# Joining the paired fp32 insertions in the mixers: keys, queries and pooling products turned and multiplied two at a time

## The chip, the cores and the metric

The kernel runs on one core of one Trainium2 chip. The metric is the time of the device in microseconds for one execution, as the median of several runs. Everything is float32 at the interface; the large products are made in fp32r from a high and a low part of each operand (x = hi + lo, three products hi·hi, hi·lo, lo·hi), the small ones in plain fp32.

## The reference

A sequence of 256 tokens with 1024 features goes through two layers of one kind and one layer of another. A layer of the first kind is a gated feed-forward block, a mixer, and a second feed-forward block. Cut to what matters here, its mixer is:

```python
z = rms_norm(x, mix_norm) @ w_in
u, q, k, v, gl = split(z)                    # 512, 512, 512, 512, 2048 columns
y_pool = multiscale_pool(u, pool_w, pool_scale)   # per group g of 4: (mean over window - u_g) @ pool_w[g]
q = rope(rms_norm(q)); k = rope(rms_norm(k)) # per head of 64
y_attn = softmax attention of 8 heads(q, k, v)
merged = gates0 * (y_pool @ w_branch_pool) + gates1 * (y_attn @ w_branch_attn)
x = x + merged @ w_out
```

The layer of the second kind has a larger mixer (an mLSTM branch beside a compressed, a selected and a windowed attention) and one feed-forward block with a convolution.

## The kernel before

The program has eight stages in a row: `L0f1 L0 L0f2 L1f1 L1 L1f2 M Mf`. `L0` and `L1` are the mixers of the first kind ("mixers one and two"), `M` is the third mixer, and the others are feed-forward blocks. The weights stream in tiles of 128x1024; ScalarE copies each into its high part (`whi`, L1369), VectorE subtracts it for the low part (`wlo`, L1976), and TensorE multiplies both with the activations `hx`.

Each of the five engines has a program of its own, written out by hand, and they meet in semaphores. Inside a mixer a counter of **beats** sets the order: after every piece of a tile's product each engine's own `tick()` raises its counter and puts in the small work that is listed for that number. The beat only fixes the place in the engine's own instruction stream; it does not make engines meet. In mixers one and two the beats are: 1 to 8 the product for q, 9 to 16 the four blocks for u (two each), 17 to 24 the product for v (four tiles, two token halves each), and 25 onward the gate blocks.

The small work that matters here, in mixers one and two:
- `turn_qk(a, isq)` on TensorE (helper `turn4`, all at L1094): four 128x128 transposes of half a of the rotated keys or queries (`ro`, a part of `gates`) into bank 4+a. It waits until VectorE has added the two parts of the rotation (`rp_add`, L2330). ScalarE moves the result to `kT1` or `qT1` (`turned`, L1700 and L1698).
- `pool_mix(g)` on TensorE (L1137): the pooling product of group g, one fp32 matmul with 256 columns that the chip runs as two matmul instructions, into bank 6 for even g and bank 7 for odd g. It waits until VectorE has the pooled difference (`pl_d`, last written at L2355). ScalarE then writes its high part (L1706, `yphi`), and VectorE its low part (`pool_mix` of VectorE's program, L2359, which raises `yplo`). Since groups 2 and 3 write the banks of groups 0 and 1, TensorE's `pool_mix(g)` for g of 2 or 3 waits for the low part of g - 2:

```python
if g >= 2:
    E.wait_ge("yplo", 4 * l + g - 1)
```

- VectorE's own ticks put the low parts of the pooling at its beats 15, 17, 20 and 23, the additions of the queries at 15 and 16, and the pooled differences at 10, 12, 14 and 16:

```python
if beat in (15, 17, 20, 23):
    pool_mix((15, 17, 20, 23).index(beat))
if beat in (15, 16):
    add(beat - 15, 1)
if beat in (10, 12, 14, 16):
    pool_diff((beat - 10) // 2)
```

- At beat 26 the attention begins on TensorE (`scores`, L1030), which waits for all keys, queries and the last `yplo`.

In the third mixer `turn_q(a)` (beats 24 and 25) does the same for its queries, and `mlstm_turn(a)` (beats 74 and 76) transposes the output of the mLSTM branch into banks 2 and 3; ScalarE and VectorE take it out again at L1842 and L2552, and the first product of the merge waits for both.

Of the kernel before, what the change touches and what calls it, by code (L numbers as in the profile page):

```python
# [228 lines left out]
ML = 46  # L229
# [182 lines left out]
def build_program(nc, x_in, wstream, gains, const_in, par_in, out, cat, pat, plan, addends):  # L412
# [3 lines left out]
    with ExitStack() as ctx:  # L416
# [285 lines left out]
        def pe_program(E):  # L702
# [412 lines left out]
            def mixer1(s, l):  # L1115
                tag = STAGES[s]
                js = jobs1(l)
                beat = 0

                def turn_qk(a, isq):  # L1120
                    if isq:
                        E.wait_ge("rp_add", 4 * l + 2 + a + 1)
                        E.wait_ge("kt_ev", 2 * l + a + 1)
                    else:
                        E.wait_ge("x", 4 * (s - 1) + a + 1)
                        E.wait_ge("rp_add", 4 * l + a + 1)
                        E.wait_ge("ld_c", 16)
                    turn4([ro[:, a * 512 + c * P:a * 512 + c * P + P] for c in range(4)], side[a]).then_inc(sem["qkt_t"], 1)

                def pool_mix(g):  # L1130
                    E.wait_ge("pl_d", PLD(l, g))
                    E.wait_ge("ld_pw", 32 * l + 32)
                    if g >= 2:
                        E.wait_ge("yplo", 4 * l + g - 1)
                    else:
                        E.wait_ge("x", 4 * (s - 1) + 3 + g)
                    e.matmul(side[2 + g % 2][:, 0:S], pw[:, (3 - g) * P:(4 - g) * P], u4[:, 3 - g, 16:16 + S], start=True, stop=True).then_inc(sem["pl_w"], 1)  # L1137

                def before(i):
                    if i < 2:  # L1140
                        E.wait_ge("kt_ev", 2 * l + 2)
                        E.wait_ge("qt_ev", 2 * l + 2)
                        E.wait_ge("yplo", 4 * l + 4)
                    else:
                        E.wait_ge("v_ev", 2 * l + 2)

                def tick():
                    nonlocal beat
                    beat += 1
                    if beat in (10, 12):  # L1150
                        turn_qk((beat - 10) // 2, False)
                    if beat in (22, 24):
                        turn_qk((beat - 22) // 2, True)
                    if beat in (18, 20, 22, 24):
                        pool_mix((beat - 18) // 2)
                    attention(l, beat, 26, js, before)

                first_group(s, f"{tag}k")
                group(f"{tag}q", 512, tick)
                for f in range(4):  # L1160
                    feat_block(T[f"{tag}u{f}"], claim((f"{tag}u", f))[:, 0:S], tick=tick)
                group(f"{tag}v", 512, tick)
                for f in range(KD):
                    for j in range(2):
                        wide_block(T[f"{tag}g{j}{f}"], claim((f"{tag}g", f, j)), tick)
                merge_tail(s, l)

            def mixer2(s):
# [14 lines left out]
                def turn_q(a):  # L1183
                    E.wait_ge("rp_add", 10 + a + 1)
                    E.wait_ge("kc2_ev", 4 * a + 4)
                    turn4([ro[:, a * 512 + c * P:a * 512 + c * P + P] for c in range(4)], side[a]).then_inc(sem["qkt_t"], 1)
# [105 lines left out]
                def tick():  # L1292
                    nonlocal beat
                    beat += 1
                    if 10 <= beat <= 13:
                        turn_k(beat % 2, beat < 12)
                    if beat in (24, 25):
                        turn_q(beat - 24)
                    if beat == 16:
                        gate_rows()  # L1300
                    attention(2, beat, 29, js, before)
                    if beat in (31, 34, 36, 38, 44):
                        compressed((31, 34, 36, 38, 44).index(beat))
                    if beat in range(ML, ML + 24, 6):
                        mlstm_scores((beat - ML) // 6)
                    if beat in MLO:
                        mlstm_out(MLO.index(beat))
                    if beat in (ML + 28, ML + 30):
                        mlstm_turn((beat - ML - 28) // 2)

                def conv_in(f):
                    feat_block(T[f"Mqk{f}"], claim(("Mqk", f))[:, 0:S], tick=tick)
# [32 lines left out]
        def act_program(E):  # L1345
# [329 lines left out]
            def mixer1(s, l):  # L1675
# [32 lines left out]
                def tick():  # L1708
                    nonlocal beat
                    beat += 1  # L1710
                    if beat in (10, 12):
                        turned((beat - 10) // 2, 0)
                    if beat in (22, 24):
                        turned((beat - 22) // 2, 1)
                    if beat in (18, 20, 22, 24):
                        pool_mix((beat - 18) // 2)
                    attention(l, beat, 26, js)

                norm_hi(s, 1)
# [35 lines left out]
            def mixer2(s):  # L1755
# [17 lines left out]
                def turned_q(a):  # L1773
                    E.wait_ge("qkt_t", 8 + a + 1)
                    e.activation(qT2.rearrange("p (k t) -> p k t", t=S)[:, :, a * P:a * P + P], by4(side[a][:, :]), ACT.Copy).then_inc(sem["qt_ev"], 1)
# [68 lines left out]
                def tick():  # L1844
                    nonlocal beat
                    beat += 1
                    if 10 <= beat <= 13:
                        turned_k(beat % 2, beat < 12)
                    if beat == 18:
                        logf()  # L1850
                    if beat in (24, 25):
                        turned_q(beat - 24)
                    if beat == 26:
                        exp_m()
                    if beat in CONV:
                        conv_end(CONV.index(beat))
                    if beat == 28:
                        compressed(0)
                    attention(2, beat, 29, js)
                    if beat in (31, 34):  # L1860
                        compressed((31, 34).index(beat) + 1)
                    if beat == 40:
                        compressed(3)
                    if beat == 44:
                        compressed(4)
                    if beat == ML + 1:
                        mlstm_exp(0)
                    if beat in range(ML + 6, ML + 24, 6):
                        mlstm_exp((beat - ML) // 6)
                    if beat in (ML + 8, ML + 14, ML + 20, ML + 22):  # L1870
                        mlstm_squares((ML + 8, ML + 14, ML + 20, ML + 22).index(beat))
                    if beat in (ML + 28, ML + 30):
                        mlstm_turned((beat - ML - 28) // 2)

                def conv_in(f):
                    tick()
# [90 lines left out]
        def dve_program(E):  # L1967
# [433 lines left out]
            def mixer2(s):  # L2401
# [152 lines left out]
                def tick():  # L2554
# [32 lines left out]
                        mlstm_out(MLO.index(beat))  # L2587
                    if beat == ML + 24:
                        mlstm_gate()
                    if beat in (ML + 28, ML + 30):  # L2590
                        mlstm_lo((beat - ML - 28) // 2)

                def conv_in(f):
                    tick()
# [435 lines left out]
```

## Time and profile before

| | |
|---|---|
| median of 3 runs | 1401.39 us (1401.39 to 1401.51) |
| the profiled execution: its time, its span | 1401.45 us, 1399.7 us |
| TensorE matmul busy | 1394.3 us, 7680 instructions |
| VectorE busy | 1098.7 us (78%) |
| ScalarE busy | 859.1 us (61%) |
| GpSimd busy | 225.9 us (16%) |
| mean granted clock of TensorE | 1.000 |

A matmul's start is recorded and its end is modelled, and the records of neighbours overlap; so the pace of TensorE is read from the distance of starts, not from the durations. Starts are given to 0.01 us. The span is the time between the first and the last instruction, and the execution's own time is 1.75 us more.

### The profile page before, as it was taken

What the parts mean: (1) busy time and instruction counts of PE and PEld (TensorE: products, weight loads), DVE (VectorE), ACT (ScalarE), POOL (GpSimd) and SP (SyncE); (2) the same over time, 40 slices, a digit from 0 to 9 for tenths busy, and PEclk for the clock granted to TensorE, in tenths of its full rate; (3) what the DMA queues carried; (4) which work ended last, traced back from release to release, by engine and by line L of the source; (5) the groups of instructions that cost most, each with busy time, mean ns of one, the idle gap of its engine ahead of it and who ended that gap; (6) DMA issues with size and microseconds to landing.
All of it is one profiled execution on the core that took longest, in us unless ns stands there. A gap on an engine that the chain in (4) does not pass through costs nothing.

```text
span 1399.7 us, 20305 instructions
## 1 busy us (share of the span) xinstructions
PE 1394.3 (100%) x7680; PEld 1195.7 (85%) x7680; DVE 1098.7 (78%) x1665; ACT 859.1 (61%) x1393; POOL 225.9 (16%) x309
## 2 busy tenths in 40 slices
PE   9999999999999999999999999999999999999999
PEld 7888888898888888888888988888888899888887
DVE  7878878776978878788787778788777878688776
ACT  6657655855657656676567646666567765455553
POOL 1112123000111001112050001114149200100000
PEclk9999999999999999999999999999999999999999
DMA  9999755465999859998555557999547336456551
GB/s 369 300 300 281 220 180 183 138 197 185 302 257 289 213 187 299 276 276 226 166 203 181 165 181 270 267 278 260 186 156 256 121 122 225 155 172 220 192 183 59
DMA packets 86329, 304.26 MB, mean 217 GB/s; under 512 B 11724, under 2 KB 11864, under 8 KB 86232
## 3 DMA queue, kind: packets, MB, share of 16 engines
q1 hardware_dynamic: 72120, 251.84, 51.4%
q0 software_dynamic: 13824, 50.34, 18.9%
q8 instruction: 61, 1.00, 0.3%
q10 hardware_dynamic: 288, 0.79, 0.1%
q14 instruction: 36, 0.29, 0.1%
HBM read 301.87 MB, written 1.06 MB: 216 GB/s over the span
## 4 chain that ended last, share of the span: by engine, by line
PE 99%; DMA 0%; DVE 0%; ACT 0%; issue 0%; POOL 0%; ACTq 0%; POOLq 0%
PE bank L752 18%; PE bank L759 9%; PE bank L706 9%; PE bank L707 9%; PE bank L708 9%; PE bank L931 5%; PE bank L930 5%; PE bank L934 5%; PE bank L736 4%; PE bank L743 4%; PE bank L737 4%; PE bank L773 4%; PE bank L778 3%; PE bank L774 3%; PE bank L726 1%; PE bank L1030 1%
## 5 line engine op out<-in xcount | busy, mean ns | idle before, releaser
L1976 DVE TENSOR_TENSOR wlo<-raw,whi 128x1024 fp32r<-128x1024 f32 x409 | 492.5, 1231 | 12.3 <-ACT whi L1369 12.2
L1369 ACT ACTIVATE whi<-raw 128x1024 fp32r<-128x1024 f32 x409 | 417.8, 1049 | 20.3 <-PE bank L708 13.8
L752 PE MATMUL bank<-hx,whi 128*128 128x512 f32 x1088 | 267.2, 392 | 0.0
L752 PEld LDWEIGHTS bank<-hx,whi 128*128 128x128 f32 x1088 | 200.8, 188 | 41.6 <-issue 2.0
L706 PE MATMUL bank<-whi,hid 128*128 128x512 f32 x536 | 211.1, 394 | 0.0
L707 PE MATMUL bank<-wlo,hid 128*128 128x512 f32 x536 | 209.2, 390 | 0.0
L708 PE MATMUL bank<-whi,hid 128*128 128x512 f32 x536 | 208.8, 389 | 0.0
L759 PEld LDWEIGHTS bank<-hx,wlo 128*128 128x128 f32 x1088 | 142.9, 191 | 7.6
L759 PE MATMUL bank<-hx,wlo 128*128 128x256 f32 x1088 | 145.2, 282 | 0.0
L1976 DVE TENSOR_TENSOR wlo<-gates,whi 128x1024 fp32r<-128x1024 f32 x96 | 116.2, 1220 | 7.6 <-ACT whi L1369 7.0
L708 PEld LDWEIGHTS bank<-whi,hid 128*128 128x128 f32 x536 | 100.6, 188 | 21.4
L1369 ACT ACTIVATE whi<-gates 128x1024 fp32r<-128x1024 f32 x96 | 100.5, 1056 | 28.6 <-PE bank L708 13.5
L706 PEld LDWEIGHTS bank<-whi,hid 128*128 128x128 f32 x536 | 100.8, 188 | 18.9
L707 PEld LDWEIGHTS bank<-wlo,hid 128*128 128x128 f32 x536 | 100.9, 188 | 18.4
L1398 ACT ACTIVATE hid<-prod 128x256 fp32r<-128x256 f32 x78 | 32.6, 418 | 121.9 <-DVE prod L2286 58.6
L2710 POOL DMA_DIRECT2D gates<-w_dram x64 | 55.8, 872 | 290.1 <-DVE wlo L1976 290.1
L773 PE MATMUL bank<-whi,hx 128*128 128x512 f32 (+1 forms) x220 | 86.3, 394 | 0.1
L774 PE MATMUL bank<-whi,hx 128*128 128x512 f32 (+1 forms) x220 | 84.0, 383 | 0.0
L2665 POOL TENSOR_SCALAR small<-small 128x1 f32<-128x1 f32 x15 | 10.7, 715 | 403.0 <-ACT arena L1384 403.0
L930 PE MATMUL bank<-whi,yhi 128*128 128x512 f32 x192 | 75.2, 392 | 0.0
L931 PE MATMUL bank<-whi,ylo 128*128 128x512 f32 x192 | 74.9, 390 | 0.0
L778 PE MATMUL bank<-wlo,hx 128*128 128x512 f32 (+1 forms) x220 | 66.2, 383 | 0.0
(297 smaller groups left out, 2413.8 us busy)
## 6 DMA issues: line engine op xcount, KB each, us to landing
raw<-w_dram SPq DMA_DIRECT2D x414, 512.0 KB, 4.6
gates<-w_dram POOLq DMA_DIRECT2D x64, 512.0 KB, 8.1
gates<-w_dram SPq DMA_DIRECT2D x32, 512.0 KB, 5.0
arena<-w_dram POOLq DMA_DIRECT2D x32, 512.0 KB, 8.9
arena<-w_dram SPq DMA_DIRECT2D x16, 512.0 KB, 5.3
gain<-g_dram SPq DMA_DIRECT2D x7, 512.0 KB, 3.4
out_dram<-x SPq DMA_DIRECT2D x4, 256.0 KB, 2.0
par<-p_dram SPq DMA_DIRECT2D x1, 867.0 KB, 10.1
```

The costliest lines, as they stand in the source:

```text
L706: e.matmul(psum, shi, mhi, start=first, stop=False, skip_group_check=True)
L707: e.matmul(psum, shi, mlo, start=False, stop=False, skip_group_check=True)
L708: return e.matmul(psum, slo, mhi, start=False, stop=last, skip_group_check=True)
L752: e.matmul(b[:, :], hi_of(j)[:, k * P:k * P + P], hx[:, k * 2 * S:k * 2 * S + 2 * S], start=k == 0, stop=False, skip_group_check=True)
L759: ins = e.matmul(b[:, 0:S], lo_of(j)[:, k * P:k * P + P], hiT(k), start=False, stop=k == KD - 1, skip_group_check=True)
L773: e.matmul(b[:, 0:n], hiT(k, a * P, a * P + P), w, start=k == 0, stop=False, skip_group_check=True)
L774: e.matmul(b[:, 0:n], loT(k, a * P, a * P + P), w, start=False, stop=False, skip_group_check=True)
L778: ins = e.matmul(b[:, 0:n], hiT(k, a * P, a * P + P), w, start=False, stop=k == KD - 1, skip_group_check=True)
L930: e.matmul(b[:, :], sh(k), half(hi_of(j), k), start=k == 0 and n not in (2, 4), stop=False, skip_group_check=True)
L931: e.matmul(b[:, :], sl(k), half(hi_of(j), k), start=False, stop=False, skip_group_check=True)
L1369: e.activation(hi_of(t), raw_of(t), ACT.Copy).then_inc(sem["w_hi"], 1)
L1976: e.tensor_tensor(lo_of(t), raw_of(t), hi_of(t).bitcast(F32), ALU.subtract).then_inc(sem["w_lo"], 1)
```

## The change

In mixers one and two the two transposes of the keys move from beats 10 and 12 to beat 12, those of the queries from 22 and 24 to 22, and the four pooling products from 18, 20, 22 and 24 to 18 (groups 0 and 1) and 22 (groups 2 and 3). Six insertions of fp32 work into the stream of fp32r products become three. TensorE and ScalarE get the new places; the program of VectorE is as it was, and so is GpSimd's. In the third mixer `turn_q` moves from beats 24 and 25 to 25 on both engines, and `mlstm_turn` from 74 and 76 to 76, here on TensorE, ScalarE and VectorE.

```diff
@@ TensorE, mixers one and two
-                    if beat in (10, 12):
-                        turn_qk((beat - 10) // 2, False)
-                    if beat in (22, 24):
-                        turn_qk((beat - 22) // 2, True)
-                    if beat in (18, 20, 22, 24):
-                        pool_mix((beat - 18) // 2)
+                    if beat in (12, 22):
+                        for a in range(2):
+                            turn_qk(a, beat == 22)
+                    if beat in (18, 22):
+                        for g in range(2):
+                            pool_mix(2 * (beat == 22) + g)
@@ TensorE, mixer three
-                    if beat in (24, 25):
-                        turn_q(beat - 24)
+                    if beat == 25:
+                        for a in range(2):
+                            turn_q(a)
...
-                    if beat in (ML + 28, ML + 30):
-                        mlstm_turn((beat - ML - 28) // 2)
+                    if beat == ML + 30:
+                        for a in range(2):
+                            mlstm_turn(a)
@@ ScalarE, mixers one and two
-                    if beat in (10, 12):
-                        turned((beat - 10) // 2, 0)
-                    if beat in (22, 24):
-                        turned((beat - 22) // 2, 1)
-                    if beat in (18, 20, 22, 24):
-                        pool_mix((beat - 18) // 2)
+                    if beat in (12, 22):
+                        for a in range(2):
+                            turned(a, beat == 22)
+                    if beat in (18, 22):
+                        for g in range(2):
+                            pool_mix(2 * (beat == 22) + g)
@@ ScalarE, mixer three: turned_q at 25 alone, mlstm_turned at ML + 30 alone
@@ VectorE, mixer three: mlstm_lo at ML + 30 alone
```

Since the beats are numbers, the rows show best what moves. TensorE in mixer one, before: the transposes of the queries (L1094, banks 4 and 5) and the pooling products of groups 2 and 3 (L1137, banks 6 and 7) stand on both sides of the last pair of token halves of v (L773, L774, L778).

```order
854 L1094 MATMUL bank4<-cst,gates 128x128 [waits s_kt_ev,s_rp_add]
855 L1094 MATMUL bank4<-cst,gates 128x128 x3
856 L1137 MATMUL bank6<-arena 128x256 [waits s_yplo,s_pl_d]
```

```order
868 L1094 MATMUL bank5<-cst,gates 128x128 [waits s_kt_ev,s_rp_add]
869 L1094 MATMUL bank5<-cst,gates 128x128 x3
870 L1137 MATMUL bank7<-arena 128x256 [waits s_yplo,s_pl_d]
871 L752 MATMUL bank2<-hx,whi 128x512 [waits s_w_hi,s_u_ev]
```

The same place in the changed kernel:

```order
854 L1094 MATMUL bank4<-cst,gates 128x128 [waits s_kt_ev,s_rp_add]
855 L1094 MATMUL bank4<-cst,gates 128x128 x3
856 L1094 MATMUL bank5<-cst,gates 128x128 [waits s_kt_ev,s_rp_add]
857 L1094 MATMUL bank5<-cst,gates 128x128 x3
858 L1137 MATMUL bank6<-arena 128x256 [waits s_yplo,s_pl_d]
859 L1137 MATMUL bank7<-arena 128x256 [waits s_yplo,s_pl_d]
860 L773 MATMUL bank0<-whi,hx 128x512 [waits s_w_hi]
```

The second half of the queries and group 3, with its wait for `yplo`, now stand twelve matmuls of v earlier.

VectorE in mixer one, the same in both kernels (rows of the one before). L2359 with bank 6 or 7 is what raises `yplo`:

```order
665 L2359 SCALAR_TENSOR_TENSOR ylo<-bank6,par,yhi 128x256 [waits s_yphi]
666 L2330 TENSOR_TENSOR gates<-gates 128x512 [waits s_rp_c,s_rp_s] x2
667 L2349 TENSOR_TENSOR arena<-arena 128x271 [waits s_pl_d,s_u_ev]
668 L2353 TENSOR_TENSOR arena<-arena 128x2 [waits s_pl_d]
669 L2355 SCALAR_TENSOR_TENSOR arena<-arena 128x256 [waits s_pl_d]
670 L1976 TENSOR_TENSOR wlo<-raw,whi 128x1024 [waits s_w_hi]
671 L2359 SCALAR_TENSOR_TENSOR ylo<-bank7,par,yhi 128x256 [waits s_yphi]
```

Nothing moved here: the low part of group 1 (bank 7) still comes behind the additions of the queries, the pooled difference of group 3 and one split of a weight tile.

## Rows read from the trace of the kernel before

**Rows 1.** The page: TensorE's busy time, and the chain that ended last, by engine

```profile
PE 1394.3 (100%) x7680; PEld 1195.7 (85%) x7680; DVE 1098.7 (78%) x1665; ACT 859.1 (61%) x1393; POOL 225.9 (16%) x309
...
PE 99%; DMA 0%; DVE 0%; ACT 0%; issue 0%; POOL 0%; ACTq 0%; POOLq 0%
```

**Rows 2.** The waits of TensorE: us in total, times, longest

```profile
PE bank L1333 <- POOL arena L2840: 1.0, 1, 1.0
PE bank L726 <- DVE arena L1994: 0.9, 1, 0.9
```

**Rows 3.** Timeline of TensorE, blocks for u in mixer one: start us, us

```profile
213.45 0.60 PE L1094 MATMUL bank<-cst,gates 128*128 128x128 f32 x4
...
216.76 0.60 PE L1094 MATMUL bank<-cst,gates 128*128 128x128 f32 x4
...
220.07 0.28 PE L736 MATMUL bank<-hx,whi 128*128 128x256 f32 x1
...
222.95 0.40 PE L773 MATMUL bank<-whi,hx 128*128 128x512 f32 x1
```

**Rows 4.** Timeline of TensorE, the product for v in mixer one

```profile
225.70 0.59 PE L1137 MATMUL bank<-arena 128*128 128x256 f32 x2
...
228.90 0.59 PE L1137 MATMUL bank<-arena 128*128 128x256 f32 x2
...
232.10 0.60 PE L1094 MATMUL bank<-cst,gates 128*128 128x128 f32 x4
...
232.54 0.60 PE L1137 MATMUL bank<-arena 128*128 128x256 f32 x2
...
235.71 0.60 PE L1094 MATMUL bank<-cst,gates 128*128 128x128 f32 x4
...
236.14 0.60 PE L1137 MATMUL bank<-arena 128*128 128x256 f32 x2
```

**Rows 5.** Timeline of TensorE, two token halves of q in mixer one

```profile
205.14 0.39 PE L773 MATMUL bank<-whi,hx 128*128 128x512 f32 x1
...
207.86 0.39 PE L773 MATMUL bank<-whi,hx 128*128 128x512 f32 x1
```

**Rows 6.** VectorE in mixer one: three rows of its timeline, one stretch by engines (after span: PE, PEld, DVE, ACT, POOL busy)

```profile
224.58 0.92 DVE L2355 SCALAR_TENSOR_TENSOR arena<-arena 128x256 f32<-128x256 f32 x1
...
230.71 1.28 DVE L2330 TENSOR_TENSOR gates<-gates 128x512 f32<-128x512 f32 x2
...
234.05 0.47 DVE L2359 SCALAR_TENSOR_TENSOR ylo<-bank,par,yhi 128x256 fp32r<-128x256 f32 x1
...
222.00:240.00 18.00, 18.00 (x96) 15.20 (x96) 17.54 (x27) 10.03 (x16) 3.94 (x6) 1.00 0.47 158
```

**Rows 7.** The same place in mixer two: timelines of TensorE and VectorE

```profile
735.82 0.60 PE L1094 MATMUL bank<-cst,gates 128*128 128x128 f32 x4
...
737.75 0.48 DVE L2359 SCALAR_TENSOR_TENSOR ylo<-bank,par,yhi 128x256 fp32r<-128x256 f32 x1
```

**Rows 8.** Start of the program: timelines of TensorE and VectorE

```profile
1.03 3.57 PE L1333 MATMUL bank<-arena 128*128 128x128 f32 x15 [1.03 <-POOL arena L2840]
...
5.75 0.83 PE L1333 MATMUL bank<-arena 128*128 128x128 f32 x6
...
8.89 0.73 PE L794 MATMUL bank<-whi,hx 128*128 128x512 f32 x2 [0.18 <-DVE hx L2640]
...
8.15 0.69 DVE L2640 CAST hx<-bank 128x512 fp32r<-128x512 f32 x1
```

**Rows 9.** Mixer three: ScalarE and TensorE behind the query transposes, VectorE and TensorE behind the mLSTM ones

```profile
1062.05 0.60 ACT L1775 ACTIVATE arena<-bank 128x512 f32<-128x512 f32 x1 [0.32 <-PE bank L1094]
...
1065.01 0.93 PE L1030 MATMUL bank<-arena 64*128 64x128 f32 x8
...
1162.90 0.69 DVE L2552 TENSOR_TENSOR ylo<-bank,yhi 128x512 fp32r<-128x512 f32 x1 [1.63 <-ACT yhi L1842]
...
1167.54 0.64 PE L743 MATMUL bank<-yhi,wlo 128*128 128x256 f32 x4
```

More of the change, by code:

```diff
@@ L1850, in tick @@
                         logf()
-                    if beat in (24, 25):
-                        turned_q(beat - 24)
+                    if beat == 25:
+                        for a in range(2):
+                            turned_q(a)
                     if beat == 26:
@@ L1871, in tick @@
                         mlstm_squares((ML + 8, ML + 14, ML + 20, ML + 22).index(beat))
-                    if beat in (ML + 28, ML + 30):
-                        mlstm_turned((beat - ML - 28) // 2)
+                    if beat == ML + 30:
+                        for a in range(2):
+                            mlstm_turned(a)
                 def conv_in(f):
@@ L2589, in tick @@
                         mlstm_gate()
-                    if beat in (ML + 28, ML + 30):
-                        mlstm_lo((beat - ML - 28) // 2)
+                    if beat == ML + 30:
+                        for a in range(2):
+                            mlstm_lo(a)
                 def conv_in(f):
```

## The prediction

> **What bounds the kernel.** I read the page first, then TensorE's waits, then the timelines of TensorE and VectorE side by side around the moved work. TensorE is busy for the whole span and makes up 99% of the chain that ended last [rows 1]; it waits for another engine only in the first 9 us [rows 2]. So time goes away only if TensorE issues faster, and every wait the change puts on it is added in full: nothing behind it has slack to take it back. Whatever ScalarE and VectorE do sooner or later counts only where TensorE then stands still.
>
> **What an insertion costs now.** The change removes no matmul; it can only save what TensorE loses at the seams between fp32r products and fp32 work. The seams are read from distances of starts.
> - A block for u without an insertion takes 222.95 - 220.07 = 2.88 us; with four transposes it takes 216.76 - 213.45 = 3.31 [rows 3]. The insertion costs 0.43 us, some 0.109 per transpose.
> - Two token halves of q take 207.86 - 205.14 = 2.72 us [rows 5]. For v, with one pooling product in front, they take 228.90 - 225.70 = 3.20 [rows 4], so the product costs 0.48. Behind transposes the same product and pair take 235.71 - 232.54 = 3.17 [rows 4], so 0.44 of it are its own two matmuls.
> - Transposes directly in front of a pooling product take 232.54 - 232.10 = 0.44 us [rows 4], the same as alone, although they have one seam less. The whole insertion of beat 22 costs 235.71 - 232.10 - 2.72 = 0.89, against 0.43 + 0.48 = 0.91 for the two apart. A seam is therefore worth 0.02 us for a transpose group, and at most 0.05 for a pooling product.
>
> **Terms of the sum, gains.** In each of mixers one and two three seams go: one at beat 10 (0 to 0.02), one at beat 20 (0.02 to 0.05), one at beat 24 (0.02 to 0.05). That is about 0.1 us per mixer. What is saved ahead of beat 22 only makes TensorE arrive sooner at the wait below and is lost there. In mixer three two seams go, 0 to 0.1 us together; I take 0.03.
>
> **Terms of the sum, waits.** The new places are checked one by one.
> - Beat 12, keys. Both halves are added before 216.76, since TensorE turned both by then without waiting, so no wait. VectorE's next need of the first half comes behind both.
> - Beat 18, pooling 0 and 1. Group 1 stood 3.2 us later. Its difference is finished at 224.58 + 0.92 = 225.50 [rows 6]; TensorE is ready for it at 225.70 + 0.22 = 225.92 [rows 4]. No wait, with 0.4 us to spare.
> - Beat 22, second half of the queries. The additions are ready at 230.71 + 1.28 = 231.99 [rows 6]; TensorE wants the second at 232.10 + 0.44 = 232.54 [rows 4]. No wait, 0.5 us to spare.
> - **Beat 22, pooling 3.** It writes bank 7 and must wait until VectorE has taken the low part of group 1 out of it. That instruction starts at 234.05 and ends at 234.05 + 0.47 = 234.52 [rows 6]. Before, TensorE came there at 236.14 and found it done. Beat 22 itself begins where it did, since as much work stands in front of it as before. Now pooling 3 comes after eight transposes and pooling 2: 232.10 + 8 x 0.109 + 0.44 = 233.41. Will VectorE be there sooner, since ScalarE can now deliver the high part of group 1 three microseconds earlier? No: VectorE is 17.54 us busy in the 18.00 us around it [rows 6], its order did not move, and what stands ahead of L2359 are query additions, the difference of group 3 and a weight split, none of them released by moved work. It is the length of its own queue that sets 234.52.
>
> The latency from VectorE's end to TensorE's start is 8.89 - (8.15 + 0.69) = 0.05 us [rows 8]. So pooling 3 starts at 234.58 instead of 233.41: a standstill of 1.17 us. The end result, by the next fixed point: behind pooling 3 now come the last two token halves of v, 235.71 - 232.54 = 3.17 us with the product [rows 4], so the gate blocks begin at 237.75; before they began 0.43 behind 236.14, at 236.57. The mixer loses **1.18 us**, the seam of beat 24 already in it. The first weight load behind a standstill cannot be fetched under the previous matmul. That may add 0 to 0.15; I take 0.05.
>
> Mixer two has the same picture: its beat 22 starts at 735.82, its VectorE instruction ends at 737.75 + 0.48 = 738.23 [rows 7]; 738.28 - (735.82 + 0.87 + 0.44) = 1.15 us.
>
> What is behind the waiting matmul: v's last pair, then the gates, all 1.2 us later, and ScalarE, which stands at L1706 for group 3 about 1 us and splits the next weight tile later. That tile is four tiles ahead of TensorE's use, and VectorE comes to its low part only about 4 us later, so TensorE does not see it. Nor does VectorE wait at its remaining two low parts: ScalarE has group 2 by about 234.2 and group 3 by 235.7, VectorE's turns come at about 235.6 and 238.2. The attention's start needs the last low part at 238.7, TensorE comes at about 240.6.
>
> Mixer three. The queries: ScalarE takes the second half out at 1062.05 [rows 9]; with the first half now directly ahead of it that becomes 1062.1, and it is wanted at 1065.01 [rows 9]. The mLSTM turns: VectorE's second low part starts at 1162.90 and ends at 1163.59 [rows 9]; both halves now pass through ScalarE and VectorE one behind the other, which moves this to about 1163.9, and the first merge product, whose low-part matmuls are at 1167.54 [rows 9] and whose high-part ones start about 1 us before, wants it at 1166.6. Some 2.7 us to spare. Both cost nothing; if a cover were gone, it would cost the lateness, at most 0.3.
>
> **Sum**, against the profiled execution's 1401.45 us: +1.18 +1.15 +2 x 0.05 -0.03 = +2.4 us, 1403.85. The median of the runs is 0.06 lower, which gives **1403.8 us**, 0.17% more. A measurement of this kernel tells about 0.2% (2.8 us) from no change, so this is within no change, near its upper edge.
>
> **Rivals.**
> - *Seams only, no standstill* (chance 0.07). If the standstill did not occur, because VectorE's queue ran earlier than I think, the seams would give -0.2 to -0.3 us: 1401.2. Against it: VectorE's busy share and unchanged order. For a gain beyond 0.2% eight seams would each have to be worth 0.35 us; rows 3 and 4 give 0.05.
> - *The standstill is dearer by its restart, or VectorE is later* (0.20). Each 0.2 us per mixer adds 0.4; from 0.2 more per mixer on the result is slower by over 0.2%. With 0.3 more each: +3.0, 1404.4.
> - *The clock falls* (0.05), the mechanism on the other side. Place: beat 22, where TensorE now does 0.87 us of transposes, 0.44 of pooling, then 1.17 of nothing, in one row. At the program's start 128-column matmuls come 3.15 / 14 = 0.22 us apart for the first 15, and (0.83 - 0.27) / 5 = 0.11 apart for the last six [rows 8]: the first ran at the pace of 1.2 GHz, the last at that of 2.4, and the slow pace held for some 4 us. If the clock fell for as long in both mixers, half of it lost each time, 2 x 2 us more: 1407.8. It decides from a single fall on (+4.4). Against it: the granted clock is 1.00 in the stretch around beat 22 [rows 6] with 0.9 us of insertion in it, and TensorE stood still 0.9 us and 0.18 us between 6.6 and 8.9 [rows 2, 8], and the pair of 512-column matmuls behind took 0.73 us, not the 1.2 of the slow pace. On this the Trainium skill speaks against the change: "TensorE: Matmul & The Clock Gate", Part 4, says that transposes do not keep the clock gate open the way matmuls do, and its section on why this matters warns of idle gaps between bursts of matmuls. By that page transposes and standstill together would count as one gap, and the time would be the 1407.8 of this rival; the trace agrees in so far as it can only for the short gap at the start, where there was no fall, and no row here shows transposes and a standstill in one.
>
> **How the numbers follow.** My forecast, the standstill of 1.1 to 1.3 us in each of mixers one and two, has 0.68, and its own range is 1403.4 to 1404.2. The range 1402.4 to 1404.8 adds most of the dearer restart and the case that one mixer's wait is half as long, and leaves out seams alone and the clock. Slower by over 0.2% (above 1404.2): the dearer restart (0.16 of it) and the clock (0.05), with the edge of my own case, 0.24. Faster by over 0.2%: 0.02. Within: 0.74.
>
> **What the profile will show.** Right: in TensorE's waits a new row, L1137 released by VectorE's L2359 (or its new line number), 2 times, 1.1 to 1.3 us each, at about 233.4 and 737.1; the fp32r pace before and behind as now; no wait at beats 12 and 18; mixer three without one. VectorE's two low parts of group 1 at the same times as now within 0.1 us. Wrong: no such wait; a wait of the attention's first scores; an fp32r pace of 0.45 us per 512 columns behind beat 22; or a span that differs from 1399.7 by more than the two waits.

## The result, and the profile after

| | before | after |
|---|---|---|
| median (lowest to highest, runs) | 1401.57 us (1401.39 to 1401.96, 16) | 1404.35 us (1403.87 to 1404.74, 16) |
| the profiled execution: time, span | 1401.45, 1399.7 us | 1404.03, 1402.2 us |
| mean granted clock | 1.000 | 1.000 |

The ratio is 1.0019, with a 95% interval of 1.0013 to 1.0026: 2.78 us more, where the prediction said 1403.8 us and a range of 1402.4 to 1404.8. It is just under the 0.2% that it called no change. It also lies above 1404.2, the top of my own forecast's range: 0.18 us of that is the kernel before, which takes 1401.57 here and 1401.39 in the runs I started from; the rest is looked for below.

The page of the changed kernel, TensorE's busy time and the chain that ended last, answers to [rows 1]. TensorE has no more work than before, but the chain now passes through VectorE. Its 4% are not the cost: from each standstill the chain runs back over a long stretch in front of it, 35 us in mixer one and most of it VectorE's.

```profile
PE 1394.9 (99%) x7680; PEld 1195.8 (85%) x7680; DVE 1097.9 (78%) x1665; ACT 859.5 (61%) x1393; POOL 226.0 (16%) x309
...
PE 94%; DVE 4%; issue 1%; ACT 1%; DMA 0%; POOL 0%; DVEq 0%; ACTq 0%; POOLq 0%
```

The waits of TensorE in the changed kernel (us in total, times, longest) answer to [rows 2]. One row is new, the foreseen one. Lines below the edit have moved: L2363 is the L2359 of before.

```profile
PE bank L1137 <- DVE ylo L2363: 2.2, 2, 1.1
PE bank L1335 <- POOL arena L2845: 1.0, 1, 1.0
PE bank L726 <- DVE arena L1998: 0.6, 1, 0.6
```

TensorE's timeline in mixer one (start us, us, and in brackets the idle time before) answers to [rows 4]:

```profile
225.48 1.02 PE L1137 MATMUL bank<-arena 128*128 128x256 f32 x4
...
231.84 1.03 PE L1094 MATMUL bank<-cst,gates 128*128 128x128 f32 x8
232.71 0.60 PE L1137 MATMUL bank<-arena 128*128 128x256 f32 x2
234.43 0.67 PE L1137 MATMUL bank<-arena 128*128 128x256 f32 x2 [1.12 <-DVE ylo L2363]
234.75 0.58 PE L773 MATMUL bank<-whi,hx 128*128 128x512 f32 x1
...
237.70 1.07 PE L752 MATMUL bank<-hx,whi 128*128 128x512 f32 x4
```

And VectorE's timeline there answers to [rows 6]:

```profile
230.46 1.28 DVE L2334 TENSOR_TENSOR gates<-gates 128x512 f32<-128x512 f32 x2
231.66 0.43 DVE L2353 TENSOR_TENSOR arena<-arena 128x271 f32<-128x271 f32 x1
...
232.32 0.43 DVE L2359 SCALAR_TENSOR_TENSOR arena<-arena 128x256 f32<-128x256 f32 x1
232.67 1.22 DVE L1980 TENSOR_TENSOR wlo<-raw,whi 128x1024 fp32r<-128x1024 f32 x1
233.80 0.48 DVE L2363 SCALAR_TENSOR_TENSOR ylo<-bank,par,yhi 128x256 fp32r<-128x256 f32 x1
```

VectorE goes through its list as before, 0.25 us earlier, since the whole execution runs 0.22 us ahead after a shorter opening. The low part ends at 233.80 + 0.48 = 234.28. TensorE was ready for pooling 3 at 232.71 + 0.44 = 233.15 and starts it at 234.43: it lost 1.28 us. (The row says 1.12, since the modelled end of the matmul in front lies 0.16 later than the point where the next could have started.) Then 234.75 - 234.43 = 0.32 us pass to the start of the next product. In the kernel before, with no wait in front of the pooling product, it is 232.79 - 232.54 [rows 4] = 0.25, so the restart costs 0.07. The line of the kernel before:

```profile
232.79 0.58 PE L773 MATMUL bank<-whi,hx 128*128 128x512 f32 x1
```

The weight loads go with it. Before, the load of the pooling product starts 0.11 us ahead of its matmul; behind the standstill, at 234.40, it starts 0.03 ahead:

```profile
232.43 0.30 PEld L1137 LDWEIGHTS bank<-arena 128*128 128x128 f32 x2
...
234.40 0.30 PEld L1137 LDWEIGHTS bank<-arena 128*128 128x128 f32 x2 [1.50 <-issue]
```

The first line is of the kernel before, the second of the changed one.

Mixer two answers to [rows 7]. TensorE's timeline:

```profile
737.75 0.60 PE L1137 MATMUL bank<-arena 128*128 128x256 f32 x2
739.46 0.67 PE L1137 MATMUL bank<-arena 128*128 128x256 f32 x2 [1.11 <-DVE ylo L2363]
```

Lost: 739.46 - (737.75 + 0.44) = 1.27 us.

**Where the 2.6 us between the two profiled executions lie.** I laid the starts of the same matmuls of both over each other. The distance, after minus before, is -0.22 us when mixer one begins (the wait at L726 was 0.6 us, not 0.9, which differs from run to run), -0.22 behind beat 12, -0.27 at beat 22, +1.10 behind beat 22's standstill, +1.11 before mixer two, +2.40 behind it, +2.42 before mixer three and +2.56 behind it. So mixer one cost 1.32, mixer two 1.29, mixer three 0.14, and the rest of the program 0.05. Without the shorter opening this is 2.8, as the medians say.

### The profile page after: what moved, and what is told of

Read it like the earlier page. It is cut to its first block, busy times and chain, and to the rows that moved or that the text cites. A ratio compares the mean times of both kernels' runs of the same rounds, so it can differ in the third digit from the quotient of the medians.

```text
span 1402.2 us, 20305 instructions
## 1 busy us (share of the span) xinstructions
PE 1394.9 (99%) x7680; PEld 1195.8 (85%) x7680; DVE 1097.9 (78%) x1665; ACT 859.5 (61%) x1393; POOL 226.0 (16%) x309
## 4 chain that ended last, share of the span: by engine, by line
PE 94%; DVE 4%; issue 1%; ACT 1%; DMA 0%; POOL 0%; DVEq 0%; ACTq 0%; POOLq 0%
PE bank L752 18%; PE bank L759 9%; PE bank L706 9%; PE bank L707 9%; PE bank L708 9%; PE bank L931 5%; PE bank L930 5%; PE bank L934 5%; PE bank L736 3%; PE bank L743 3%; PE bank L737 3%; PE bank L773 3%; PE bank L778 3%; PE bank L774 3%; DVE wlo L1980 1%
## 5 line engine op out<-in xcount | busy, mean ns | idle before, releaser
L773 PE MATMUL bank<-whi,hx 128*128 128x512 f32 (+1 forms) x220 | 85.9, 392 | 0.0
L774 PE MATMUL bank<-whi,hx 128*128 128x512 f32 (+1 forms) x220 | 84.0, 383 | 0.0
L778 PE MATMUL bank<-wlo,hx 128*128 128x512 f32 (+1 forms) x220 | 66.1, 383 | 0.0
```

The lines of the kernel that those rows point to most:

```text
L773: e.matmul(b[:, 0:n], hiT(k, a * P, a * P + P), w, start=k == 0, stop=False, skip_group_check=True)
L774: e.matmul(b[:, 0:n], loT(k, a * P, a * P + P), w, start=False, stop=False, skip_group_check=True)
L778: ins = e.matmul(b[:, 0:n], hiT(k, a * P, a * P + P), w, start=False, stop=k == KD - 1, skip_group_check=True)
```

## The experiments

All were compared with the kernel before on the same chip; its medians there were 1401.55 to 1401.72 us. Edits are shown against the changed kernel unless said otherwise.

**1. Is it the low part of group 1 that sets the standstill?** VectorE's beats for the low parts of the pooling, one way and the other: group 1 ahead of the second query addition, or behind one more weight split.

```diff
@@ low1_early
-                    if beat in (15, 17, 20, 23):
-                        pool_mix((15, 17, 20, 23).index(beat))
+                    if beat in (15, 16, 20, 23):
+                        pool_mix((15, 16, 20, 23).index(beat))
@@ low1_late
+                    if beat in (15, 19, 20, 23):
+                        pool_mix((15, 19, 20, 23).index(beat))
```

> The changed kernel, but VectorE takes the low part of pooling group 1 out at its beat 16 instead of 17: ahead of the second query addition, the difference of group 3 and a weight split. Theory (TensorE's third-from-last waiting place is bank 7 at beat 22, and nothing else costs): yplo 2 is then there at about 231.6 instead of 234.5, the two waits of 1.1 us go, and all of the 2.8 us come back: 1401.3 to 1401.6 us. The second query addition and the difference of group 3 come 0.4 us later, just when TensorE wants them, so 0 to 0.1 us per mixer may stay as another wait. Rival (eight transposes and two pooling products in one piece, or the clock, cost by themselves): the time stays above 1403. Rival (the standstill only moves to the difference of group 3): about half stays, 1402.8.

Measured: 1401.78 us (1401.53 to 1402.16), ratio 1.0002 (0.9993 to 1.0010), 0.19 us above the kernel before on that chip. The loss is gone as far as the medians can tell. TensorE's waits have no row for L1137 any more. VectorE's timeline, and behind it TensorE's:

```profile
231.32 0.48 DVE L2363 SCALAR_TENSOR_TENSOR ylo<-bank,par,yhi 128x256 fp32r<-128x256 f32 x1
...
232.98 0.42 DVE L2359 SCALAR_TENSOR_TENSOR arena<-arena 128x256 f32<-128x256 f32 x1
```

```profile
232.97 1.19 PE L1137 MATMUL bank<-arena 128*128 128x256 f32 x4
233.81 0.58 PE L773 MATMUL bank<-whi,hx 128*128 128x512 f32 x1
```

The low part is out of bank 7 by 231.80. From the two pooling products to the next product it takes 0.84 us, where the pair of beat 18 in the changed kernel takes 226.15 - 225.48 = 0.67: pooling 3 is now late by the difference of group 3, which ends at 232.98 + 0.42 = 233.40. That is the next in line, and it costs 0.17 us. Over each mixer the distance to the kernel before grows by about 0.11, so the trace still has a small part of the loss.

> The changed kernel, but VectorE takes the low part of group 1 out at its beat 19 instead of 17: one more weight split (1.13 us of VectorE's time) stands ahead of it. Theory: each of the two standstills grows by 1.1 us, from 1.1 to 2.25, and the time by 2.3 us, to 1406.6. Rival (the clock falls once the standstill with the insertion in front is long enough): 512-column matmuls behind it 0.43 us apart for a while and 1408 or more. Rival (the wait is not what the time hangs on): 1404.4 as the changed kernel.

Measured: 1408.31 us (1408.10 to 1409.40), ratio 1.0049 (1.0036 to 1.0062). The standstills grew as they should. Waits of TensorE:

```profile
PE bank L1137 <- DVE ylo L2363: 4.5, 2, 2.3
```

That is 2.3 us more than in the changed kernel, as the theory had it, but the median is 4.0 us above it: here the rival of the clock came true. TensorE's timeline behind the standstill of mixer one, and the stretches around (after span: busy time of PE, PEld, DVE, ACT, POOL; then the granted clock):

```profile
235.57 1.19 PE L1137 MATMUL bank<-arena 128*128 128x256 f32 x2 [2.27 <-DVE ylo L2363]
236.20 0.99 PE L773 MATMUL bank<-whi,hx 128*128 128x512 f32 x1
236.99 0.63 PE L774 MATMUL bank<-whi,hx 128*128 128x512 f32 x1
237.42 0.63 PE L773 MATMUL bank<-whi,hx 128*128 128x512 f32 x1
...
238.98 0.39 PE L773 MATMUL bank<-whi,hx 128*128 128x512 f32 x1
239.21 0.39 PE L774 MATMUL bank<-whi,hx 128*128 128x512 f32 x1
```

```profile
230.00:235.00 5.00, 3.31 (x19) 2.52 (x17) 4.93 (x10) 1.88 (x4) 0.00 (x0) 1.00 0.36 112
235.00:238.00 3.00, 2.43 (x6) 1.99 (x7) 3.00 (x5) 1.20 (x2) 0.00 (x0) 0.56 0.88 264
238.00:241.00 3.00, 3.00 (x13) 2.43 (x12) 1.61 (x3) 1.28 (x3) 0.00 (x0) 0.87 0.98 330
241.00:244.00 3.00, 3.00 (x24) 2.60 (x24) 0.00 (x0) 2.37 (x3) 0.00 (x0) 1.00 0.70 268
```

The products come 0.42 us apart instead of 0.23: the granted clock fell to the lower of its two levels, 1.2 GHz, behind the standstill, and came back some 3 us later. Each fall costs about 1.5 us. In the profiled execution (1409.40 us, mean clock 0.998) it fell in both mixers. The four others (1408.1 to 1408.4 us, mean clock 0.999) have no trace; their times and clocks fit one fall each.

**2. Is it the place of pooling 3?** The joined transposes and pooling 0 and 1 stay; pooling 3 goes back to beat 24, pooling 2 stays at 22 (on TensorE and ScalarE).

```diff
-                    if beat in (18, 22):
-                        for g in range(2):
-                            pool_mix(2 * (beat == 22) + g)
+                    if beat in (18, 22, 24):
+                        for g in {18: (0, 1), 22: (2,), 24: (3,)}[beat]:
+                            pool_mix(g)
```

> The changed kernel, but the pooling product of group 3 goes back to beat 24; the eight query transposes and group 2 stay joined at beat 22. Theory: the whole loss hangs on that one matmul; TensorE comes to it at about 236.1, as before the change, finds bank 7 free, no wait: 1401.3 to 1401.6 us. Rival (the piece of eight transposes costs): above 1402. Rival (seams are worth something): below 1401.2.

Measured: 1401.88 us (1401.13 to 1401.94), ratio 1.0001 (0.9992 to 1.0009), no row for L1137 in the waits. In the trace the distance to the kernel before goes from +0.37 to +0.32 at beat 22 and stands at +0.36 behind mixer one; over mixer two it falls by 0.04. The median is 0.29 us above the kernel before, too little to tell; the opening of the trace alone is 0.37 us late. So a single pooling product moved by two beats made all of the loss that the medians can tell, and the other joins are worth 0.01 to 0.04 us per mixer.

**3. Mixer three by itself.** The changed kernel with the insertions of mixers one and two as before, on TensorE and in the same way on ScalarE.

```diff
-                    if beat in (12, 22):
...
-                    if beat in (18, 22):
...
+                    if beat in (10, 12):
+                        turn_qk((beat - 10) // 2, False)
+                    if beat in (22, 24):
+                        turn_qk((beat - 22) // 2, True)
+                    if beat in (18, 20, 22, 24):
+                        pool_mix((beat - 18) // 2)
```

> Only the part of the change in mixer three; mixers one and two as before. Theory: two seams of fp32 transposes are worth nothing, no wait comes or goes by the move: within 0.15 us of the kernel before, 1401.5. Rival (the 0.15 us that the changed kernel lost in mixer three in its trace belong to the move, through ScalarE's later eviction of the queries and the small compression products that wait for it): 1401.7 and the same 0.15 in its trace.

Measured: 1401.69 us (1401.51 to 1402.22), ratio 1.0002 (0.9993 to 1.0011). No difference that the medians can tell. The trace shows the 0.15 us of the rival: the distance to the kernel before goes from -0.10 ahead of mixer three to +0.06 behind it, 0.08 of it in one step at the compress product (L1231), which is taken up in experiment 7.

**4. Half of it.** The joins in mixer one alone, mixers two and three as before.

```diff
-                    if beat in (12, 22):
+                    joined = l == 0
+                    if beat in ((12, 22) if joined else (10, 12, 22, 24)):
...
-                    if beat in (18, 22):
+                    if beat in ((18, 22) if joined else (18, 20, 22, 24)):
```

> The change in mixer one only (keys at 12, pooling 0 and 1 at 18, queries and pooling 2 and 3 at 22); mixers two and three as before. Theory: each of the two mixers carries its own standstill, so half of the loss: one wait of 1.1 us, +1.3 us in the trace, 1402.9. Rival (the first standstill shifts the transfers so that the second mixer's is a consequence of it): either nothing or all of the 2.8.

Measured: 1402.94 us (1402.74 to 1406.46), ratio 1.0013 (1.0003 to 1.0022), 1.4 us over the kernel before, half of 2.78. One wait of 1.1 us at L1137 in mixer one, none in mixer two. The profiled execution was the 1406.46; its surplus lies ahead of the mixer and is told with the clock below. Two more executions took 1404.40; they have no trace, and what made them longer stays open.

**5. What a seam is worth.** Against the kernel *before*: each of its transpose groups is cut into two pairs, the second pair one beat later, which gives eight seams more.

```diff
+                def turn_half(a, part):
+                    for c in (2 * part, 2 * part + 1):
+                        ins = e.transpose(side[a][:, c * P:c * P + P], ro[:, a * 512 + c * P:a * 512 + c * P + P], ident)
...
+                    if beat in (11, 13, 23, 25):
+                        turn_half({11: 0, 13: 1, 23: 0, 25: 1}[beat], 1)
```

> The kernel before, with each of the four transpose groups of mixers one and two cut in two pieces of two transposes, one beat apart (second pieces at 11, 13, 23 and 25): eight seams more in all, no work more. Theory: a seam between fp32r products and fp32 transposes costs 0 to 0.02 us, so 0 to 0.16 us, 1401.6. Rival (seams cost, and the change's saving is only hidden by its standstill): 0.1 us or more each, 1402.4.

Measured: 1402.34 us (1402.15 to 1402.54), ratio 1.0003 (0.9994 to 1.0013), 0.8 us more. But the waits have a row that the kernel before has not, and TensorE's timeline in the blocks for u shows the seams themselves:

```profile
PE bank L1030 <- DVE ylo L2367: 0.5, 2, 0.2
```

```profile
213.66 0.38 PE L1132 MATMUL bank<-cst,gates 128*128 128x128 f32 x2
...
215.31 0.38 PE L1132 MATMUL bank<-cst,gates 128*128 128x128 f32 x2
...
216.96 0.27 PE L1132 MATMUL bank<-cst,gates 128*128 128x128 f32 x1
```

The attention's first scores now wait 0.24 us for the last low part in each mixer, 0.5 of the 0.8. That the late pairs bring this about, by way of ScalarE and VectorE, is argued and not shown. A whole block with two seams takes 216.96 - 213.66 = 3.30 us; with one seam it took 3.31 [rows 3]. A seam between fp32r products and transposes costs nothing here. My expectation had no place for the wait at L1030; as a price of seams the total alone would have misled.

**6. When does the clock fall?** The rival of the prediction had the transposes in front count as part of the gap. So I put the standstill where only fp32r products stand in front, at beat 24, and made it longer in two steps, with VectorE's low parts of groups 1 and 2 (then also 3) held back.

```diff
@@ wait_at_24, VectorE; TensorE and ScalarE as in experiment 2
+                    if beat in (15, 23, 24):
+                        for g in {15: (0,), 23: (1, 2), 24: (3,)}[beat]:
+                            pool_mix(g)
@@ wait_at_24_longer
+                    if beat in (15, 25):
+                        for g in {15: (0,), 25: (1, 2, 3)}[beat]:
+                            pool_mix(g)
```

> Pooling 3 back at beat 24, the eight query transposes left at 22, and VectorE's low parts of groups 1 and 2 only at its beat 23, behind four weight splits in a row: the same kind of standstill (1.9 to 2.1 us), but behind a whole pair of token halves of fp32r products and not behind a piece of fp32 work. Theory on the clock (the standstill of 2.3 us brought the clock down only together with the 1.3 us of transposes and pooling in front of it): granted clock 1.00 throughout, +2.1 us per mixer, 1405.8. Rival (the standstill alone does it): stretches at 0.5 behind it, up to 1.6 us more per mixer, 1407 to 1409.

Measured: 1405.10 us (1405.08 to 1405.92), ratio 1.0027 (1.0016 to 1.0038), mean clock 1.000 in every execution. The standstill came out at 1.8 us by the row, shorter than the 1.9 to 2.1 expected and than the 2.3 of low1_late, so this run alone doesn't decide between theory and rival. TensorE's timeline, mixer one:

```profile
237.89 0.67 PE L1137 MATMUL bank<-arena 128*128 128x256 f32 x2 [1.77 <-DVE ylo L2363]
238.21 2.19 PE L752 MATMUL bank<-hx,whi 128*128 128x512 f32 x8
240.23 1.11 PE L759 MATMUL bank<-hx,wlo 128*128 128x256 f32 x8
```

> As the one before, but VectorE's low parts of groups 1 to 3 only at its beat 25, one more split later: a standstill of 3.0 to 3.3 us behind fp32r products, longer than the 2.3 us that brought the clock down behind transposes. Theory on the clock (only together with fp32 work in front): no stretch at 0.5, +3.3 per mixer, 1408.2. Rival (length of the standstill alone): stretches at 0.5 in both mixers, 1410 to 1412.

Measured: 1410.79 us (1410.63 to 1411.19), ratio 1.0066 (1.0051 to 1.0081), mean clock 0.998 in all four executions. TensorE's timeline and stretches, mixer one:

```profile
239.17 0.67 PE L1137 MATMUL bank<-arena 128*128 128x256 f32 x2 [2.90 <-DVE ylo L2363]
239.49 3.73 PE L752 MATMUL bank<-hx,whi 128*128 128x512 f32 x8
243.01 1.19 PE L759 MATMUL bank<-hx,wlo 128*128 128x256 f32 x8
```

```profile
237.00:240.00 3.00, 0.83 (x3) 0.74 (x4) 2.42 (x4) 0.12 (x1) 0.00 (x0) 0.96 0.93 287
240.00:243.00 3.00, 3.00 (x8) 2.34 (x7) 0.48 (x1) 2.98 (x5) 0.00 (x0) 0.50 0.96 366
243.00:246.00 3.00, 3.00 (x27) 2.42 (x26) 0.88 (x6) 0.61 (x2) 0.00 (x0) 0.97 0.11 40
```

Eight products of 512 columns take 243.01 - 239.49 = 3.52 us instead of 240.23 - 238.21 = 2.02. So the fall costs 1.5 us again, and a standstill of this length needs no transposes in front: the rival came true. Mixer two shows the same. The lengths of standstill in the mixers, and the one long one at an opening:

| standstill by the wait row | in front of it | granted clock behind |
|---|---|---|
| 1.1 us (changed kernel, both mixers) | eight transposes, one pooling product | 1.00 |
| 1.8 us (wait_at_24, both) | fp32r products | 1.00 |
| 2.3 us (low1_late, both) | eight transposes, one pooling product | 0.5 in one mixer or both |
| 2.9 us (wait_at_24_longer, both) | fp32r products | 0.5 |
| 2.88 us (opening, mixer_one_alone_at_22) | thirty 128-column fp32 matmuls | 0.5 |

The last is the profiled execution of experiment 4. Its opening wait was 2.88 us, not 0.9; the same wait in the other traces, up to 1.3 us, left the clock at 1.00. Timeline of TensorE and stretches:

```profile
9.85 1.94 PE L726 MATMUL bank<-cst,arena 128*128 128x128 f32 x8 [2.88 <-DVE arena L1996]
```

```profile
9.00:12.00 3.00, 2.15 (x9) 1.85 (x10) 2.36 (x4) 1.17 (x2) 0.00 (x0) 0.56 1.03 421
12.00:15.00 3.00, 3.00 (x8) 2.07 (x9) 3.00 (x4) 3.00 (x7) 0.25 (x1) 0.50 1.03 415
```

**7. Both costs taken away, and mixer three once more.** Mixer three as in the kernel before, in the changed kernel and in low1_early.

```diff
-                    if beat == 25:
-                        for a in range(2):
-                            turn_q(a)
+                    if beat in (24, 25):
+                        turn_q(beat - 24)
...
-                    if beat == ML + 30:
-                        for a in range(2):
-                            mlstm_turn(a)
+                    if beat in (ML + 28, ML + 30):
+                        mlstm_turn((beat - ML - 28) // 2)
```

> Both costs taken away: VectorE's low part of group 1 one beat earlier, and mixer three as it was before; what stays of the change is the joined insertions of mixers one and two. Theory (the 2.8 us of the change are the two standstills behind pooling 3, some 2.6, and some 0.1 in mixer three): against the kernel before, the seams saved are worth 0 to 0.1 us and the rest of the standstill costs 0.1 per mixer: 1401.4 to 1401.8, no row of TensorE waiting at L1137, and mixer three without a shift. Rival (the joined insertions cost something besides the standstill, for example in ScalarE's longer row of evictions): 1402.2 or more. Rival (seams are worth more than I read from the starts, 0.1 us each): 1400.9 or less, and then this version beats both kernels.

Measured: 1401.92 us (1401.25 to 1402.20), ratio 1.0001 (0.9992 to 1.0010), 0.1 above the theory's range on a chip where the kernel before took 1401.72. None of the versions tried beats the kernel before; the standstill for the difference of group 3 costs more than the 0.05 us that beats 18 and 20 save, and the mixers are 0.13 and 0.09 us longer than before. That is the theory, and the rival of seams worth 0.1 us falls.

> The change without its part in mixer three. Theory (mixer three costs some 0.1 us, which comes to TensorE at the compress product L1231 through ScalarE and GpSimd): 0.1 us below the changed kernel, 1404.2 to 1404.4, too little for the medians to tell, but in the trace the distance of TensorE's starts to those of the kernel before stays within 0.03 us from the joined query turns of mixer three to its end, where the changed kernel loses 0.08 at L1231. Rival (the 0.1 of mixer three has nothing to do with the joined turns, it comes with any later start of the mixer): the step of 0.08 at L1231 is there as well.

Measured: 1404.27 us (1403.74 to 1404.47), ratio 1.0019 (1.0010 to 1.0028), 0.1 under the changed kernel, as expected but too little to tell. The trace speaks against my theory, though: mixer three is 0.13 us longer than before here too, with the step at L1231, although its turns stand where they stood. What goes with the step is GpSimd. Timelines at the compress product, the kernel before:

```profile
1078.24 0.39 PE L774 MATMUL bank<-whi,hx 128*128 128x512 f32 x1
...
1078.34 0.21 POOL L2825 MEMSET small<- 128x128 f32 x1
...
1079.47 0.66 PE L1231 MATMUL bank<-small,cst 128*128 128x64 f32 x4
```

and the changed kernel with mixer three as before:

```profile
1080.44 0.39 PE L774 MATMUL bank<-whi,hx 128*128 128x512 f32 x1
...
1080.60 0.20 POOL L2825 MEMSET small<- 128x128 f32 x1
...
1081.74 0.66 PE L1231 MATMUL bank<-small,cst 128*128 128x64 f32 x4
```

GpSimd comes to its memset 0.10 us behind the product in the one and 0.16 in the other, and L1231, which waits through ScalarE for what follows it, 1.23 and 1.30 us behind. In low1_early_m3_before it is 0.09 and 1.22, in the changed kernel and in mixer3_alone 0.17 to 0.18 and 1.31 to 1.32. All seven kernels of this study with joined turns in mixer three show the step (0.06 us or more); of the four without, this one shows it, seams_doubled half of it (0.04), and two don't. So the joined turns may shift GpSimd, but they are not needed for it, and what else does stays open; it is 0.07 us. Most of what is left of mixer three's surplus, 0.05 us, has already arisen by 1049 us, some 10 us ahead of the first edited instruction of this mixer. It is there in the changed kernel, in mixer3_alone and as much in low1_early_m3_before, whose mixer three has no edit, so it doesn't come from the turns.

## Why the prediction was right, and where it was off

- **The mechanism.** The prediction put the loss on one row, pooling 3 waiting for the low part of group 1, twice. That row is there, with 1.12 and 1.11 us. Taking it away by either of its two ends (VectorE's order, TensorE's place) leaves 0.2 and 0.3 us of the 2.78, which the medians can't tell from nothing; doubling it makes the time grow. The argument that ScalarE's earlier delivery would not bring VectorE forward, because VectorE's own queue sets the time, held to 0.03 us.
- **"No wait" at beats 12, 18 and for the second query half.** Right: no such row, and the distance of the two traces does not move at beats 12 and 18.
- **The size of the standstill.** The term was 1.17 + 0.05 in mixer one. Measured: 1.28 lost, and 0.07 for the restart. The step that was undersized is the latency from VectorE's end to TensorE's start: taken as 0.05 us from the opening [rows 8], it is 234.43 - 234.28 = 0.15 here. The kernel before had the right one too, at the longer wait of its opening, 7.48 - (6.58 + 0.75) = 0.15:

```profile
6.58 0.75 DVE L1994 SCALAR_TENSOR_TENSOR arena<-x,small,gain 128x512 f32<-128x512 f32 x1 [0.74 <-POOL small L2667]
...
7.48 1.23 PE L726 MATMUL bank<-cst,arena 128*128 128x128 f32 x8 [0.90 <-DVE arena L1994]
```

The restart, taken as 0.05 out of 0 to 0.15 without a row, is 0.32 - 0.25 = 0.07. Another 0.03 us lies in the two token halves behind it in mixer one and in no such place in mixer two; it stays open. With the seams' gain taken off, mixer one lost 1.32 and mixer two 1.29, against my 1.23 and 1.20: 0.18 us in sum.
- **Mixer three.** The term was -0.03, and the profiled difference is +0.14. I looked for lateness at the two places that the edit touches and found none, rightly. Of the 0.14, 0.05 arose ahead of the edit, and 0.07 to 0.08 arose 17 us behind the query turns at L1231 through GpSimd, which shares no row of the change; experiment 7 shows that this comes without the edit too. 0.17 us off.
- **The sum.** -0.18 and -0.17 account for most of the 0.4 us between 2.4 predicted and 2.78 measured; the rest is within what the medians leave. So the rival "dearer restart" was partly true: 0.08 to 0.09 us more per mixer, nearly all of it in the release and not in the restart, and below the 0.2 from which it would have made the result slower by over 0.2%. One sign that I had named as wrong is met if the waits are taken from their rows: the span is 2.5 us longer, and the rows have 2.2. Counted from the starts, 1.28 + 1.27 = 2.55, it is not.
- **The seams.** Taken as 0.02 for transposes and up to 0.05 for a pooling product. Measured 0.00 at beat 12, 0.00 in experiment 5, 0.05 for beats 18 and 20 together. The rival "seams only" had their size right and failed on the standstill.
- **The clock.** The rival did not occur at 1.1 us, but its mechanism is real, and its price was too high: 1.5 us per fall, not 2. I had let transposes and standstill count together, following "TensorE: Matmul & The Clock Gate", Part 4, of the Trainium skill, which says that transposes do not keep the clock gate open the way matmuls do. That both together would be enough was my reading and not the words of the Trainium skill, and the changed kernel's trace does not agree with it: 1.31 us of fp32 insertion and 1.28 of nothing in a row, and a granted clock of 1.00. The warning of the Trainium skill in the same page's section on why this matters, of idle gaps between bursts of matmuls, agrees with the traces in kind: 2.9 us of standstill alone let it fall in both mixers. Whether transposes in front make a 2.3 us standstill fall that would otherwise not was not tried.

## What to carry to other kernels

Before joining insertions on the engine that bounds a kernel, list for each piece moved forward what it waits for, and ask when that engine's queue comes to it, not when its input could be ready: here a product moved by two beats met a buffer that VectorE freed 1.1 us later, and every gain of the join was smaller than a tenth of that. Price a standstill as its lateness plus about 0.2 us for release and restart, and count a second, larger price, about 1.5 us here, if it gets long: here it came at 2.3 us and not at 1.8, and nothing between them was measured. Take the latency from a wait as long as the one you expect. If such a join is wanted all the same, move the release with it: one number in VectorE's list took back all of the loss but 0.2 us.

## What the runs showed of the hardware

- The granted clock fell behind standstills of 2.3 and 2.9 us and not behind 1.1 and 1.8. The fall shows near the standstill's end, not at its start: in mixer one of low1_late the two fp32 matmuls behind it are slow already (236.20 - 235.57 = 0.63 us, against 0.32 in the changed kernel), in wait_at_24_longer they take 239.49 - 239.17 = 0.32 and the products after them are slow. And low1_late lost it in both mixers in one execution and, by their times and mean clocks, in one mixer in the four others.
- A seam between fp32r products and a group of fp32 transposes cost nothing that starts given to 0.01 us can show.
- Where TensorE had stood 0.2 us or longer for VectorE (L726, L1030 and L1137, in all traces here), it started 0.15 us behind the end of the VectorE instruction, the same at the opening as in the mixers. Where it had stood 0.18 to 0.19 us (L794 at the opening, in nine traces), it started 0.05 us behind. Why the short wait differs stays open.
